# Bidirectional hybrid encoder trunk: square sums added in pairs on VectorE, and three activation-table preloads taken out

## What is computed

```python
def rmsnorm(x, g):
    return x * lax.rsqrt(jnp.mean(x * x, axis=-1, keepdims=True) + EPS) * g
...
for l in range(DEPTH):
    mix = hybrid_mixer(rmsnorm(h, norm_mix_pre[l]), ...)      # LRU group and GLA group
    h = h + rmsnorm(mix, norm_mix_post[l])
    ff = squared_relu_mlp(rmsnorm(h, norm_mlp_pre[l]), w_mlp_up[l], w_mlp_down[l])
    h = h + rmsnorm(ff, norm_mlp_post[l])
```

## Time and profile before

| | |
|---|---|
| median of 3 runs | 2679.28 us (2679.07 to 2680.3) |
| profiled execution, its own time | 2679.07 us |
| its span, first to last instruction | 2677.1 us |
| mean granted TensorE clock | 0.945 |
| PE / PEld busy | 95% / 90% |
| DVE / POOL / ACT busy | 37% / 34% / 21% |
| activation-table loads | 39 |

### The profile page before, as it was taken

How to read it: one execution, slowest core, us unless ns; L and a number is a source line. 1 busy time by engine, 2 the same in 40 slices (tenths; PEclk the granted TensorE clock), 3 DMA queues, 4 the chain that set the end, 5 groups by cost and what they waited for, 6 DMA issues and landing times.

```text
span 2677.1 us, 35954 instructions
## 1 busy us (share of the span) xinstructions
PE 2531.1 (95%) x15144; PEld 2409.1 (90%) x15144; DVE 990.5 (37%) x917; ACT 568.4 (21%) x701; POOL 910.5 (34%) x553
## 2 busy tenths in 40 slices
PE   7889999989999999999988999999899999999995
PEld 5888977969999999999868889689699999999995
DVE  4678232172222212221577672322722122222226
ACT  3553122131100100010234531321401000100111
POOL 8223210374333333333372222104723333333331
PEclk9888976999999999999999989679999999999998
DMA  5100100141111111111231011001411111111113
GB/s 181 40 24 32 47 17 1 56 138 45 48 41 46 47 47 47 47 63 41 78 111 38 24 39 36 12 17 52 132 48 48 47 47 41 45 47 47 63 48 112
DMA packets 60899, 143.18 MB, mean 53 GB/s; under 512 B 5136, under 2 KB 36112, under 8 KB 60816
## 3 DMA queue, kind: packets, MB, share of 16 engines
q1 hardware_dynamic: 28368, 99.20, 10.5%
q10 hardware_dynamic: 32448, 42.77, 5.1%
HBM read 120.57 MB, written 21.38 MB: 53 GB/s over the span
## 4 chain that ended last, share of the span: by engine, by line
PE 81%; DVE 9%; POOL 5%; issue 4%; ACT 1%; ACTq 0%; DMA 0%; DVEq 0%; POOLq 0%; SPq 0%
PE banks L404 69%; PE banks L668 4%; POOL x_gained L333 2%; POOL X L337 2%; DVE xc L1163 1%; PE banks L430 1%; PE banks L640 1%; PE banks L631 1%; PE banks L454 1%; PE banks L566 1%; DVE T L1136 1%; DVE xc L1159 1%; DVE acc L1045 1%; PE banks L726 1%; DVE hh L1136 0%
## 5 line engine op out<-in xcount | busy, mean ns | idle before, releaser
L404 PE MATMUL banks<-X,w_hl 128*128 128x348 f32 (+1 forms) x7920 | 1295.8, 325 | 0.4 <-DVE vT L1032 0.4
L404 PEld LDWEIGHTS banks<-X,w_hl 128*128 128x128 f32 x7920 | 1275.0, 190 | 9.1 <-issue 6.2
L317 POOL TENSOR_SCALAR w_hl<-w_raw 128x1024 fp32r<-128x1024 f32 x180 | 194.7, 1082 | 1614.9 <-PE banks L404 1341.4
L404 PE MATMUL banks<-act_hi,w_hl 128*128 128x348 f32 x3024 | 563.5, 321 | 0.0
L319 POOL TENSOR_TENSOR w_hl<-w_raw,w_hl 128x1024 fp32r<-128x1024 f32 x180 | 504.9, 2805 | 15.0
L404 PEld LDWEIGHTS banks<-act_hi,w_hl 128*128 128x128 f32 x3024 | 494.2, 188 | 0.0
L1004 ACT ACTIVATE T<-T 128x1044 f32<-128x1044 f32 x64 | 69.0, 1079 | 1196.3 <-DVE T L1369 1196.3
L404 PE MATMUL banks<-act_lo,w_hl 128*128 128x348 f32 x1512 | 321.3, 321 | 0.0
L1369 DVE SCALAR_TENSOR_TENSOR T<-banks,rs 128x1044 f32<-128x1044 f32 x64 | 79.7, 1246 | 591.5 <-PE banks L404 573.5
L1390 DVE TENSOR_TENSOR Y<-banks,Y 128x1044 f32<-128x1044 f32 x96 | 119.6, 1246 | 374.0 <-PE banks L404 374.0
L404 PEld LDWEIGHTS banks<-act_lo,w_hl 128*128 128x128 f32 x1512 | 253.9, 188 | 0.0
(11 more groups left out here) (175 smaller groups left out, 1911.6 us busy)
## 6 DMA issues: line engine op xcount, KB each, us to landing
w_raw<-w_units SPq DMA_DIRECT2D x184, 512.0 KB, 3.2
h_old<-h_out ACTq DMA_DIRECT2D x24, 348.0 KB, 3.6
h_mid<-Y ACTq DMA_DIRECT2D x24, 348.0 KB, 4.2
h_old<-h_mid ACTq DMA_DIRECT2D x24, 348.0 KB, 3.9
h_out<-Y ACTq DMA_DIRECT2D x24, 348.0 KB, 4.2
Y<-x_in ACTq DMA_DIRECT2D x6, 696.0 KB, 10.2
h_out<-Y ACTq DMA_DIRECT2D x6, 696.0 KB, 6.4
gates_raw<-w_gates SPq DMA_DIRECT2D x8, 256.0 KB, 2.6
```

What stands on the lines that cost most here:

```text
L317: nc.gpsimd.tensor_scalar(slot[:, 0], w_raw[:, s], 1.0, 1.0, ALU.mult, ALU.mult).then_inc(w_rounded, 1)
L404: ins = nc.tensor.matmul(out[:, b, 0:width(b)], wp, xp[:, used(b)], start=first and n == 0, stop=last and n == 2)
```

## The change

Four edits in one:

- DVE adds the two halves of each squared piece (`add_pair`), and PE makes one `ones` matmul a piece in place of two, behind the new semaphore `sq_pair`. For layer 0's first norm the twelve adds stand behind the chain of the LRU parameters; in `update` the add of piece n-1 stands behind the last operation of piece n.
- The preloads of L852, L901 and L931 are gone.
- PE no longer waits for `banks_zeroed` at its start.

```diff
@@ add_piece (PE)
-                pe.wait_ge(sq_h, sbase + n + 1)
-                nc.tensor.matmul(sum_bank(norm, b), ones[:, :], sq[:, n % SQ_RING, 0, :], start=first, stop=False)
-                nc.tensor.matmul(sum_bank(norm, b), ones[:, :], sq[:, n % SQ_RING, 1, :], start=False, stop=last)\
+                pe.wait_ge(sq_pair, sbase + n + 1)
+                nc.tensor.matmul(sum_bank(norm, b), ones[:, :], sq[:, n % SQ_RING, 0, :], start=first, stop=last)\
                     .then_inc(sum_done if last else sq_read, 1)
@@ PE, ahead of the layers
             pe.wait_ge(const_ready, 1)
-            pe.wait_ge(banks_zeroed, 2)
@@ ACT, start
             load_x(0)
-            nc.scalar.preload_act_table_set("natural_log_exp_and_others")
@@ DVE
+            def add_pair(total, n):
+                dve.wait_ge(sq_h, total + n + 1)
+                V.tensor_tensor(sq[:, n % SQ_RING, 0, :], sq[:, n % SQ_RING, 0, :], sq[:, n % SQ_RING, 1, :], ALU.add)\
+                    .then_inc(sq_pair, 1)
@@ DVE, update
                     ins.then_inc(y_new, 1)
+                    if n >= 1 and (l, phase) != (L - 1, 1):
+                        add_pair(total + NX, n - 1)
+                if (l, phase) != (L - 1, 1):
+                    add_pair(total + NX, NX - 1)
@@ DVE, behind the chain of the LRU parameters
             V.tensor_scalar(nsp, sp, -1.0, None, ALU.mult).then_inc(par_ready, 1)
+            for n in range(NX):
+                add_pair(0, n)
```

More of the change, by code:

```diff
@@ L212, in trunk_kernel @@
         x_hi, x_lo = sem("x_hi"), sem("x_lo")
+        sq_pair = sem("sq_pair")
         sq_h, sq_read = sem("sq_h"), sem("sq_read")
```

## The result

The changed kernel takes 2699.1 us (median of 10 runs, 2687.92 to 2710.42) against 2674.39 for the kernel before (10 runs, 2667.11 to 2680.3): ratio 1.0087, interval 1.0066 to 1.0108, some 23 us slower. I had forecast 2720 with a range from 2700. The profiled execution of the changed kernel took 2690.59 us by its own time, span 2688.8, mean granted clock 0.949.

What follows compares the result with a forecast made beforehand. PE was busy 95% of the span, but behind an `update` DVE and POOL taking turns set the pace. 13.5 + 3 x (5.0 + 2.0) + 5.6 + 1.2 = 41.3 us, added to 2679.07, gave 2720 us, range 2700 to 2744.

Steps and rivals of the forecast that it cites:

- First norm: Layer 0's first norm: adds behind the parameter chain start the sums late, and loads are added; `rs` +12.3 to +14.7, taken +13.5 us.
- Adds behind an `update`: Three norms behind an `update`: DVE and POOL both full, so 12 adds at 0.42 us lengthen each norm by 5.0 us.
- The bounds 0 and 0.5: Price per DVE add behind an `update`: 0 if it finds a gap, about 0.5 us if it keeps POOL out throughout.
- Tail of these norms: End of three norms: `Ln` and `Exp` loads +2.8, less 0.6 for the earlier sum and 0.2 PE tail: +2.0 us each.
- Behind the last chunk: After each layer's last GLA chunk: low halves end at 474.4, PE's matmuls last until 473.9; +0.6 a layer, 1.2 us.
- Decay gates: Loads ahead of `Exp` and `Ln` go through to DVE and PE: 2.8 us a layer, 5.6 in all.
- GLA chunks hidden: Two loads a GLA chunk lengthen ACT's chain by 2.8 us, hidden in idle time with 0.2 to spare; no cost.
- `banks_zeroed`: PE's start: the removed wait ends 14 us ahead of PE's first data, so removing it gives nothing.
- One set stays loaded: Rival: tool chain looks ahead and chooses the common `Ln` and `Exp` set, only late loads left; +24.7, 2704 us, chance 0.13.
- Sums set the pace: Rival: adds cost POOL nothing and norms follow PE's order, so 28.1 us come back; 2651 us, chance 0.03.
- A load costs twice: Rival: each table load brings a stop of its own length again, exposed loads 24 us, chunks 14; 2758 us, chance 0.04.
- The clock falls in the norms: Rival: PE drops to its lower clock in norms, 5.0 us a piece against 4.26; 27 us in all, 2747, chance 0.12.

Runs made afterwards that it cites:

- kernel 6: Kernel before plus the adds only, preloads kept, with every add behind an `update` done twice, the first into an unread scratch tile: 2714.26 us, one run.
- Kernel 2: The kernel before without its three preloads and nothing else: 2688.92 us, ratio 1.0039.
- kernel 7: The kernel before without its first two preloads, the third (behind `Silu`) kept: 2669.98 us, ratio 0.9983.
- 3: The changed kernel, but layer 0's first norm keeps two sum matmuls a piece, no adds, and the `banks_zeroed` wait: 2694.06 us, ratio 1.006.
- 4: The changed kernel with the first norm's twelve adds set between the steps of the parameter chain: 2691.01 us, ratio 1.0051.
- 8: Kernel before with ACT writing `x_gained` behind an `update`, adds between chain steps in the first norm only, preloads kept: 2655.63 us, ratio 0.9905.
- kernel 5: Kernel before, but ACT writes `x_gained` in norms behind an `update` and POOL only the low halves; no adds: 2657.08 us, ratio 0.9919.
- again: The kernel before, nothing edited, in a second profiled execution on a third chip: span 2677.8 us.
- 1: The changed kernel with the three preloads and the `banks_zeroed` wait put back, so the adds alone: 2690.17 us, ratio 1.005.

## Why the prediction was wrong

The step that failed is one of the path: I counted the load ahead of every `Ln` behind a last sum as late. Behind an `update` it runs inside the wait for that sum, and so it does at the first `Ln` of the first norm and behind layer 1's last chunk. Next to it the price of an add was mis-sized, and two things that the sum did not have, the base and stages that vary, took the rest. In the order of the sum:

- **First norm, 13.5 forecast, 12.1 and 10.5 found** (each pair of executions). The steps came as told: PE idle until 28.59, lower level until 34, two loads behind the last sum, `Exp` at 66.29 where it was 54.22. The first sum came 1.3 us earlier than I had, since the parameter chain did not pass on the load ahead of it, and the load of the first `Ln` ran inside a wait (35.40), so that POOL started piece 5 at 41.18 where I had 43.8. Its seven pieces then took 21.9 us, within the 19.6 to 22.4 I gave.
- **Adds behind an `update`, 5.0 a norm forecast.** The value per add was mis-sized: 0.42 taken, 0.34 found, and over eleven intervals, not twelve: 3.7 a norm, 3.8 us too much in three. The bounds 0 and 0.5 held, and kernel 6 points to what decides between them: 0.34 while POOL is full too, 0.49 in pieces where DVE alone is. The Trainium skill's rule (SBUF — State Buffer, "SBUF: two separate sides"), taken as a whole add that keeps POOL out, would have put it at the upper bound; the measured 0.34 is below that.
- **Tail of these norms, 2.0 forecast, about 0.7 found.** This is the step that failed. "`Ln` and `Exp` behind the last sum get a load each: +2.8" is false there: the load of `Ln` (610.81) runs inside the wait, and 1.28 - 0.6 = 0.7 is left. Kernel 2, with the loads alone, has the same norms 1.15 to 1.27 us longer: one load and not two. This term and the one before were 7.0 together and came out at 4.35, 4.48 and 4.32: 7.9 us too much in three norms, half for each, the largest part of the miss.
- **Behind the last chunk, 1.2 forecast, nothing found.** PE's row of layer 0 there is 86 matmuls in 14.14 us without a gap, as in the earlier trace rows:

```profile
470.12 14.14 PE L405 MATMUL banks<-X,w_hl 128*128 128x348 f32 x86
```

  The last low halves end at 475.3, 1.65 us later behind the last chunk's sum than before and not 2.8, and PE has its 36 matmuls until 476.0. In layer 1 ACT's load ahead of that `Ln` lies in a wait too:

```profile
1797.52 1.28 ACT L956 ACT_TABLE_LOAD   x1
1801.01 0.61 ACT L956 ACTIVATE o_rs<-banks,eps 128x416 f32<-128x416 f32 x1 [2.21 <-PE banks L640]
```

- **Decay gates, 5.6 forecast, 5.7 found** (2.74 + 2.99). PE's weight loads wait 2.58 us for `vT` where they waited 0.45:

```profile
288.55 1.56 PEld L405 LDWEIGHTS banks<-X,w_hl 128*128 128x128 f32 x10 [2.58 <-DVE vT L1034]
```

- **GLA chunks hidden, nothing forecast.** In this ACT timeline at the higher level `Exp` comes every 6.68 us (421.77, 428.45), the period of the earlier trace rows; both loads lie in ACT's idle time.

```profile
421.77 0.55 ACT L959 ACTIVATE o_rs<-o_rs 128x416 f32<-128x416 f32 x1
...
427.15 1.28 ACT L959 ACT_TABLE_LOAD   x1
428.45 0.55 ACT L959 ACTIVATE o_rs<-o_rs 128x416 f32<-128x416 f32 x1
```

- **`banks_zeroed`, nothing**: PE's first matmul waits for ACT's high half with the wait (kernel 7, 15.20) as without it. Its removal alone was not tried.

By its own terms the sum is then 12.1 + 13.1 + 5.7 = 30.9. The remaining step to 25.0 is time that I had not in the sum at all: LRU -1.6 and -2.5, output projection -1.6 and -1.6, and +1.2 in small parts. The projection's 1.6 is a short fall of the clock near the stage's end, there or not: the same 24 matmuls between two of PE's waits for `acc` take 5.46 us in the second execution of the changed kernel (from 561.49) and 4.22 in the first (from 555.03), 1.2 of the 1.6. In the LRU stage layer 0's -1.6 was absent in the second execution (159.89); layer 1's -2.5 came twice, and in kernels 2, 3 and 4 too (157.92 to 158.60), though the mean clock of the stage was no higher (0.91 against 0.93 before). The added loads are not the cause by themselves: kernels 6 and 8 keep all preloads and had 157.38 and 156.73. Why it is shorter is open.

The absolute number also rests on the base. I added to 2679.07 from the first runs; in ten runs the kernel before had a median of 2674.39. So 4.7 of the 21.3 us between 2720.4 and 2699.1 are the base's, and on my base the measured ratio gives 2702.4, inside the range. That the result fell outside by 0.9 us is a matter of such small shifts; that 41.3 stood for 25.0 is not.

Of the rivals none came true with its price, though 2699.1 lies near the 2704 of the first. One set stays loaded: 113 loads stand against it. Sums set the pace: only with POOL's load lightened (kernel 5). A load costs twice: the next activation starts 0.01 to 0.02 behind the load's end (64.42 behind 63.13 + 1.28, 616.75 behind 615.45 + 1.28). The clock falls in the norms: 0.97 in layer 0's, as before, but it did fall in layer 1's, to 0.84 in the stretch below and to 0.88 from 1901 to 1945, where it had been 0.95 and 1.00. Its condition came true there, its price did not: these norms took 54.05 and 53.91 beside 53.93, for POOL (43.08 busy of 44) still set the pace.

```profile
1341.00:1385.00 44.00, 33.20 (x142) 26.74 (x142) 40.04 (x40) 23.40 (x38) 43.08 (x34) 0.84 0.50 153
```

What stays open is the GLA part. In profiled executions it lay between 395.7 and 417.8 us. Set against the ratios ("left" in the table) it added between -10 and +4 us, and -2 in the changed kernel; most of these are within what the intervals allow, kernel 7's -10 is not and stays open. Which chunk gets which level was neither forecast nor steered here.

## What to carry to other kernels

A load or other preparation that stands ahead of an instruction with a wait may run inside the wait: before it is priced, look in a trace whether it lies ahead of the wait or behind it, and count only what comes behind the data. Work moved to an engine goes to a place in its queue, and the place can cost more than the work (12 adds: 8 us behind a chain, a gain between its steps). And before taking work from the busiest engine, see in the chain which engine sets the pace in that stage; here it was POOL with DVE, and lightening POOL gave 20 us in three norms where lightening PE gave only more waiting, but for 0.6 us at the end of each.

## What was not expected of the hardware

- A DVE add of 0.51 us beside a busy POOL cost 0.34 us of pace; the second one of the same size cost 0.49 in the later pieces of a norm.
- The load for the same line of the program, L763, was carried out ahead of a semaphore wait in one place (610.81, then 2.79 us of waiting) and behind it in another (63.13, after 5.22 us).
- Two executions with the same code and PE's start 0.2 us apart differed by more than 1 us in the moment when PE rose to the higher level, and the first norm with it (57.30 and 58.54).
- Kernels with the same GLA work and no loads in it took 395.7 to 416.5 us for it (7, 5 and 8), and yet four profiled executions 411.9 to 412.0 (before, again, 1 and 6).
